# RWKV's key factor on VectorE, its norms' root on GpSimd, and the weight halves' splits one step earlier

## The reference

```python
a = jax.nn.sigmoid(a0 + xa @ a2)
g = jax.nn.sigmoid(xg) @ g2
kk = heads(k * k_k)
kk = kk / jnp.maximum(jnp.sqrt(jnp.sum(kk * kk, axis=-1, keepdims=True)), 1e-12)
k = k * (1.0 + (a - 1.0) * k_a)
...
state = (state * w_t[:, :, None, :] + sa[..., None] * b_t[:, :, None, :]
         + v_t[..., None] * k_t[:, :, None, :])
```

## Time and profile before

| | |
|---|---|
| time, median of 3 runs | 1017.78 us (1017.22 to 1019.56) |
| the profiled execution | 1018.65 us, span of its instructions 1016.9 us, mean granted TensorE clock 0.985 |
| busy: PE, DVE, ACT, POOL | 954.4 us (94%), 567.7 (56%), 431.1 (42%), 223.2 (22%) |
| chain of work that ended last | PE 78%, DVE 13%, ACT 6% |
| costliest groups | L1687 ACT split and copies 238.5 us; L695, L696, L697 PE 173.6, 165.4, 165.4; L2414 DVE split 144.2 |
| ACT table loads | 10 (8 at L1683, 2 at L1684), 1283 ns each |

### The profile page before, as it was taken

The page is one execution under the profiler, slowest core; times in us unless marked ns, Lnnn a source line. Parts: engine busy times, 40 slices in busy tenths (PEclk is TensorE's granted clock), DMA queues, the critical chain, the costliest instruction groups (busy, mean ns, idle before and its releaser), DMA issues.

```text
span 1016.9 us, 15852 instructions
## 1 busy us (share of the span) xinstructions
PE 954.4 (94%) x6780; PEld 781.1 (77%) x6780; DVE 567.7 (56%) x867; ACT 431.1 (42%) x687; POOL 223.2 (22%) x151
## 2 busy tenths in 40 slices
PE   5989999989989999999899999979989989999996
PEld 3988888767558988888779977756558788888875
DVE  1458665754463444777764666844663244444883
ACT  2574234343342444546343344453441334545560
POOL 1000000100000255567420540000000024444570
PEclk9999999999989999999999999979999999999999
DMA  9344333222545765555329663313553466766531
GB/s 330 102 135 138 100 102 108 85 69 66 200 169 166 225 195 180 204 182 191 135 72 213 142 207 120 125 59 107 182 191 110 118 166 170 201 173 201 177 113 42
DMA packets 134949, 151.85 MB, mean 149 GB/s; under 512 B 15936, under 2 KB 106304, under 8 KB 134752
## 3 DMA queue, kind: packets, MB, share of 16 engines
q1 hardware_dynamic: 133952, 147.14, 46.7%
q10 hardware_dynamic: 928, 3.70, 1.0%
HBM read 149.78 MB, written 1.05 MB: 148 GB/s over the span
## 4 chain that ended last, share of the span: by engine, by line
PE 78%; DVE 13%; ACT 6%; issue 2%; DMA 1%; POOL 0%; POOLq 0%; SPq 0%; ACTq 0%; DVEq 0%
PE psum L806 10%; PE psum L695 7%; PE psum L697 7%; PE psum L696 7%; PE psum L758 6%; PE psum L807 6%; PE psum L1292 3%; PE psum L778 3%; PE psum L779 3%; PE psum L787 3%; PE psum L701 2%; PE psum L864 2%; ACT parts L1687 2%; PE psum L854 2%; PE psum L855 2%
## 5 line engine op out<-in xcount | busy, mean ns | idle before, releaser
L1687 ACT ACTIVATE parts<-low 128x1024 fp32r<-128x1024 f32 (+2 forms) x234 | 238.5, 1047 | 107.7 <-PE psum L697 65.4
L695 PE MATMUL psum<-parts 128*128 128x512 f32 (+2 forms) x424 | 173.6, 409 | 9.6 <-DVE parts L2414 6.7
L2414 DVE TENSOR_TENSOR parts<-low,parts 128x1024 fp32r<-128x1024 f32 (+2 forms) x115 | 144.2, 1262 | 51.8 <-ACT parts L1687 51.2
L696 PE MATMUL psum<-parts 128*128 128x512 f32 (+2 forms) x424 | 165.4, 390 | 0.0
L697 PE MATMUL psum<-parts 128*128 128x512 f32 (+2 forms) x424 | 165.4, 390 | 0.0
L806 PE MATMUL psum<-parts 128*128 128x512 f32 x434 | 155.7, 398 | 0.0
L1687 ACT ACTIVATE high<-psum 128x512 f32<-128x512 f32 (+5 forms) x103 | 56.3, 565 | 185.9 <-PE psum L809 73.1
L807 PE MATMUL psum<-parts 128*128 128x256 f32 x496 | 129.3, 281 | 0.0
L3227 POOL TENSOR_TENSOR parts<-low,parts 128x1024 fp32r<-128x1024 f32 x33 | 86.6, 2623 | 118.3 <-ACT parts L1687 118.3
L695 PEld LDWEIGHTS psum<-parts 128*128 128x128 f32 x424 | 80.7, 190 | 35.0 <-issue 8.2
L807 PEld LDWEIGHTS psum<-parts 128*128 128x128 f32 x496 | 93.9, 189 | 5.7
(11 more groups left out here) (305 smaller groups left out, 1500.9 us busy)
## 6 DMA issues: line engine op xcount, KB each, us to landing
low<-in_w_in_dram SPq DMA_DIRECT2D x40, 1024.0 KB, 5.2
low<-in_w_ffn_in_dram SPq DMA_DIRECT2D x44, 512.0 KB, 5.1
low<-in_w_ff_in_dram SPq DMA_DIRECT2D x16, 1024.0 KB, 5.8
low<-in_w_ff_out_dram SPq DMA_DIRECT2D x16, 1024.0 KB, 4.9
low<-in_w_ffn_out_dram SPq DMA_DIRECT2D x11, 1024.0 KB, 5.0
low<-in_w_out_dram SPq DMA_DIRECT2D x8, 1024.0 KB, 5.2
low<-in_w_ple_gate_dram SPq DMA_DIRECT2D x4, 1024.0 KB, 5.0
low<-in_w_up_dram SPq DMA_DIRECT2D x3, 1024.0 KB, 5.0
```

Of the source, the lines that this page charges most:

```text
L695: mm(o, l[0], r[0], start, False)
L696: mm(o, l[0], r[1], False, False)
L1687: return e.activation(o, a, ACT.Copy)
L2414: tt(rslot3(n, nk, width)[:, r, 0:w], slot3(n, nk, width)[:, r, 0:w], st.hi3(j)[:, r, 0:w].bitcast(F32), ALU.subtract) \
```

## The change

ScalarE no longer makes the key factor. VectorE does it with four TENSOR_SCALAR operations (multiply by k_a, add 1 - k_a) behind the maximum. The root and the reciprocal of the norms become one power with exponent -1/2 on GpSimd, and TensorE's transposes wait for that. The order of VectorE's next two products is exchanged (A4 with the decay factor first, KM with the keys behind it). In `feature_chunk` and `token_range` the first and second half of the next slot are now split at the slot's steps 1 and 2 on ScalarE and at 2 and 3 on VectorE; before, the second half came at the last step or in the middle.

```diff
@@ -985,7 +985,7 @@
                 free[b] = [rw_dve.at("n")]
                 for _ in range(4):
                     yield
-                q.wait_ge(*rw_dve.at("ni"))
+                q.wait_ge(*rw_pool.at("ni"))
                 for h in range(2):
                     b = next(rw_bank)
                     p = bank(b)
@@ -1741,8 +1741,8 @@
             def feature_chunk(st, j, widths, read):
                 steps = 1 + len(widths)
                 for n in range(steps):
-                    if n in (0, steps - 1):
-                        split(st, j + 1, (1 if n else 0,))
+                    if n < 2:
+                        split(st, j + 1, (n,))
                     yield
                 q.wait_ge(*main_pe.at(st.tag, j, 1))
                 read()
@@ -1753,8 +1753,9 @@
                 banks = [next(pg), next(pg)]
                 for s in range(n):
                     for i in range(2):
-                        split(st, j0 + s + 1, (i,))
-                        for _ in range(nk // 2):
+                        for r in range(nk // 2):
+                            if i == 0 and r < 2:
+                                split(st, j0 + s + 1, (r,))
                             yield
                         if s == n - 1:
                             q.wait_ge(*main_pe.at(st.tag, j0 + s, i))
@@ -1884,14 +1885,7 @@
                 act(Qx, Qx, ACT.Exp, scale=-S0).then_inc(rw_act.up("qx"), 1)
                 q.wait_ge(*rw_dve.at("f"))
                 act(fct, fct, ACT.Exp, scale=-S0).then_inc(rw_act.up("f"), 1)
-                q.wait_ge(*rw_act.at("a", 1, 1))
-                q.wait_ge(*init_dve.at("omka"))
-                for c in range(4):
-                    s = slice(256 * c, 256 * c + 256)
-                    act(KM[:, s], A4[:, s], ACT.Identity, scale=vec("rwkv_k_a", c), bias=omka[:, c:c + 1]).then_inc(rw_act.up("km", c), 1)
-                yield
-                q.wait_ge(*rw_dve.at("n"))
-                act(knorm, knorm, ACT.Sqrt).then_inc(rw_act.up("n"), 1)
+                yield
                 for _ in range(3):
                     yield
                 next(rw_bank), next(rw_bank)
@@ -2440,9 +2434,8 @@
                 late()
                 for n in range(1 + len(widths)):
                     yield
-                    if n == 0:
-                        split(st, j + 1, (0,))
-                split(st, j + 1, (1,))
+                    if n < 2:
+                        split(st, j + 1, (n,))
                 read()
                 yield
 
@@ -2454,7 +2447,7 @@
                         for r in range(nk // 2):
                             if (s, i, r) == (0, 0, 0):
                                 late()
-                            if r == 1:
+                            if (i, r) in ((0, 1), (1, 0)):
                                 split(st, j0 + s + 1, (i,))
                             yield
                         if s == n - 1:
@@ -2568,15 +2561,17 @@
                 p = bank(next(rw_bank))
                 q.wait_ge(*rw_pe.at("n"))
                 ts(knorm, p[:, 0:16], 1e-24, None, ALU.max, None).then_inc(rw_dve.up("n"), 1)
-                q.wait_ge(*rw_act.at("km", 3))
+                yield
+                q.wait_ge(*rw_act.at("a", 1, 1))
+                for c in range(4):
+                    s = slice(256 * c, 256 * c + 256)
+                    ts(KM[:, s], A4[:, s], vec("rwkv_k_a", c), omka[:, c:c + 1], ALU.mult, ALU.add).then_inc(rw_dve.up("km", c), 1)
+                yield
+                q.wait_ge(*rw_act.at("qi"))
+                q.wait_ge(*rw_dve.at("km", 3))
+                tt(A4, A4, Qi, ALU.mult).then_inc(rw_dve.up("aq"), 1)
+                yield
                 tt(KM, KM, zk_f, ALU.mult).then_inc(rw_dve.up("km"), 1)
-                yield
-                q.wait_ge(*rw_act.at("n"))
-                e.reciprocal(knorm, knorm).then_inc(rw_dve.up("ni"), 1)
-                yield
-                q.wait_ge(*rw_act.at("qi"))
-                tt(A4, A4, Qi, ALU.mult).then_inc(rw_dve.up("aq"), 1)
-                yield
                 yield
                 bs = [next(rw_bank) for _ in range(2)]
                 q.wait_ge(*rw_dve.at("qx"))
@@ -3329,7 +3324,10 @@
                 q.wait_ge(*rw_act.at("g", 1))
                 e.memset(H0_f, 0.0).then_inc(rw_pool.up("h0"), 1)
                 yield
-                yield from steps(14)
+                q.wait_ge(*rw_dve.at("n"))
+                tt(knorm, knorm, mh.broadcast_to([128, 16]), ALU.pow).then_inc(rw_pool.up("ni"), 1)
+                yield
+                yield from steps(13)
 
                 def normed(i):
                     yield from steps(2)
```

More of the change, by code:

```diff
@@ L2570, in rwkv @@
                 ts(knorm, p[:, 0:16], 1e-24, None, ALU.max, None).then_inc(rw_dve.up("n"), 1)
-                q.wait_ge(*rw_act.at("km", 3))
-                tt(KM, KM, zk_f, ALU.mult).then_inc(rw_dve.up("km"), 1)
                 yield
-                q.wait_ge(*rw_act.at("n"))
-                e.reciprocal(knorm, knorm).then_inc(rw_dve.up("ni"), 1)
+                q.wait_ge(*rw_act.at("a", 1, 1))
+                for c in range(4):
+                    s = slice(256 * c, 256 * c + 256)
+                    ts(KM[:, s], A4[:, s], vec("rwkv_k_a", c), omka[:, c:c + 1], ALU.mult, ALU.add).then_inc(rw_dve.up("km", c), 1)
                 yield
                 q.wait_ge(*rw_act.at("qi"))
+                q.wait_ge(*rw_dve.at("km", 3))
                 tt(A4, A4, Qi, ALU.mult).then_inc(rw_dve.up("aq"), 1)
                 yield
+                tt(KM, KM, zk_f, ALU.mult).then_inc(rw_dve.up("km"), 1)
                 yield
```

## The result

The changed kernel took 1009.32 us (median, 1007.05 to 1009.75) against 1017.50 for the kernel before beside it: ratio 0.9912 (0.9897 to 0.9927). A later comparison of the same two kernels gave 0.9875 (0.9855 to 0.9895). So it is faster by about 1%, within the range, and by about twice what was forecast (8.2 us by the medians, 9.0 by the ratio, for 4.5): this is rival A, 1009.0, the case without turn-taking.

What follows compares the result with a forecast made beforehand. TensorE, busy 94% of the span, was taken to bound the kernel. Slot 5 (0.4), the rest of stage 1 (2.9) and stage 2 (1.2) summed to 4.5 us: 1013.3 us against 1017.78, with an 8-in-10 range of 1008 to 1016.5.

Steps and rivals of the forecast that it cites:

- rival A: Slot 5, stage 1: GpSimd's power and VectorE's one-input operations don't take turns; gain 8.8, 1009.0 us (1010.5 variant); chance 0.32.
- Slot 5: Stage 1, TensorE's 3.10 us wait at 76.77: power holds VectorE's key factor, TensorE resumes at 77.9; gain 0.4.
- The half clock: TensorE: waits above 2 us bring a half-clock stretch costing 1.5; at slot 5 gain 0.4, or 1.9 without it.
- The rest of stage 1: TensorE's waits at 109.33, 172.06, 254.20 and small ones shrink or go: 1.34 + 0.42 + 0.6 + 0.5 = 2.9.
- slot 9: Stage 1, 109.33: TensorE's wait for the second half goes, as VectorE splits ahead of six decay-mask operations; 1.34.
- the load at 168.5: ScalarE's 1.28 us table load for Exp before the first attention softmax is spared; TensorE's 0.42 wait at 172.06 goes.
- Stage 2: Waits at 632.31 (0.2) and 670.60 (1.0) shrink; sum 1.2.
- the 2.27: Stage 2, 632.31: wait for slot 10's second half becomes about 1.1, nearly all absorbed by ScalarE's chain; gain 0.2.
- 670.60: Stage 2: TensorE's 5.02 wait loses 1.0 as ScalarE's split moves before the softmax exponentials; half clock behind unchanged.
- Rival B: Given back: small gains of stages 1 and 2 absorbed by other chains; 0.4 to 1.5, 1016.3 to 1017.4 us; chance 0.14.
- D: Later slots' splits are late on ScalarE, blocking z copies; four of twelve at 0.5 us, gain 2.5, 1015.3; no separate chance.
- C: Long power at slot 5 holds VectorE's key factor: slower, about 1019.4 us; decides from 7.1 us; chance 0.05.

Runs made afterwards that it cites:

- splits_only: Kernel before with only the splits' steps changed; ScalarE still makes the key factor and the root: 1012.80 us, ratio 0.9944.
- before_ct: Kernel before with only ScalarE's copy for TensorE's stage-2 wait of 5.02 us put ahead of the softmax exponentials: 1011.41 us, ratio 0.9909.
- all_first: Changed kernel with key factor and the products aq and km ahead of both splits of slot 5 on VectorE: 1010.97 us, ratio 0.9916.
- ct_early: Changed kernel with ScalarE's copy for TensorE's stage-2 wait of 4.07 us put ahead of the softmax exponentials and stick weights: 1001.60 us, ratio 0.9834.
- rwkv_only: Changed kernel with the splits' old steps, leaving key factor on VectorE and power on GpSimd: 1014.08 us, ratio 0.9956 to the kernel before.
- aq_first: Changed kernel with key factor and the product aq ahead of both splits of slot 5 on VectorE: 1008.89 us, ratio 0.9894.

## Why the prediction was wrong

*Slot 5* is the step that failed, at "it starts its work at 72.5 and ends at 75.25, and VectorE's key factor stands still meanwhile". I took a rule that the rows show for a 512-column product over to a power. The power's length I had about right (2.75 for 2.90), and also that the split holds it (3.89 in all). The direction of the hold was the error: a running power of 16 columns held neither one-input nor two-input operations of VectorE. That a hold lasts only as long as data is moved, and that the power spends its 2.9 us on something else, fits all the rows but is not shown. The rows before had a hint: a power takes 0.16 us a column, while 512 columns of a product pass in 2.2. The step cost 4.7 - 0.4 = 4.3 us of the gain, and 4.9 was measured for what rival A puts at 4.7.

*The half clock.* That its stretch goes with the wait of 3.0 to 3.1 at slot 5 held: the profiles with that wait (before, splits_only, before_ct) have it, the others don't. The rule "every wait above 2 has one" did not: the kernel before could not refute it, but all_first does, where 2.54 has none, and ct_early, where 3.51 has none. In the forecast it turned 1.9 into 0.4 at slot 5.

*The rest of stage 1.* Forecast 2.9, measured 4.2. At slot 9 it was 1.6 for a wait of 1.34; a matmul behind a wait also starts its successor later (0.22 for 0.12 at 109.33 of before). Between 110.9 and 187.8 us 1.6 came for some 0.9, and 1.0 came behind it for 0.6 and small ones. ScalarE has 8 table loads in place of 10, as forecast, and rwkv_only, which leaves the splits alone, gains 0.6 between 110.9 and 187.8, where 0.42 was put for the load at 168.5.

*Stage 2.* Forecast 1.2, measured 1.2 in the first profile and 1.7 in the second, from 620.3 to 762.6. That the 2.27 is absorbed was right: the wait at 623.12 fell to 0.97, and 1.00 for the stick operation came behind it. At 670.60 the wait shrank by 0.95, as put. But "with the half clock behind unchanged" was wrong: another 1.0 came behind the wait, where the half level in the kernel before went on longer (0.50 in 671 to 675 us and 0.60 in 675 to 679; in the changed kernel 0.61 in 664 to 668, then 1.00). And 0.9 was lost at 750, where the half level lasted about twice as long as before (0.56 in 745 to 750 us and 0.70 in 750 to 754; before 0.58 in 756 to 760, then 0.99). That the sum came out at the forecast's 1.2 is luck.

*Sum.* 4.9 + 4.2 + 1.2 = 10.3, less 1.2 for the start that was late: 9.1 in the spans. Rival A is right in its mechanism; its 8.8 came out so near because 1.3 more in stage 1 met a start that was 1.2 late. *Rival B* (given back) holds for slot 10 alone, where the ledger falls by 1.5 from 640.0 to 653.3; the rest of stage 1's and stage 2's gains stayed. Of *D* (moved splits late on ScalarE) there is no sign: no new wait of TensorE for a split appears. *C* would have needed a power of 7.1 us; it takes 2.90 by itself. One sum of the prediction is off by itself: 1013.3 less 1.5 is 1011.8, not 1011.3, as the lower end of the forecast's own range.

## What to carry to other kernels

Before a hold between two engines goes into a sum, ask whether the rows show it for this kind of instruction and this width, and in this direction: the duration of an instruction alone doesn't tell how long it holds its neighbour. The narrow power was free here on an engine that was idle, since what waits for it came later than its length plus one instruction of the neighbour. And look at each long wait of the bounding engine for a copy that stands behind work that is wanted later: moving one of 0.6 us brought 0.9% alone (before_ct, 0.9909), nearly as much as the whole change.

## What the runs showed that was not expected

- A GpSimd power costs about 0.16 us a column of 128 partitions above 0.4 (0.56, 1.65, 2.90 and 5.42 us for 1, 8, 16 and 32), waits for a two-input VectorE operation under which it starts (3.89 for 2.90), and held none that began under it. A product of 128 x 512 does hold, and it holds a TENSOR_SCALAR too (1.13 for 0.40).
- The half level of TensorE's clock does not follow from the length of a wait alone: 2.54 us without it (all_first), 3.51 us with it in the changed kernel and without it in ct_early, and waits of 0.99 and 1.08 with it (aq_first). A stretch like that at slot 5 (0.57 over 4 us) costs 1.4 to 1.6 us in the ledger (at 214, 221, 799 and 812 us); some last twice as long. Whether one comes differs between executions of code that is the same up to that place, so a stretch that comes or goes in one profile is no proof of what the edit did. What decides it stays open.
